# A hybrid decoder step on one core: queries and keys of the second mixer by 32 x 32 tiles, with the key features kept in the order the tiles leave them

## The reference, cut to what matters

```python
def headwise(u, w):          # 512 blocks of 4 features
    return jnp.einsum('btni,noi->btno', u.reshape(B, T, 512, 4), w).reshape(B, T, 2048)
q = headwise(xc, wq); k = headwise(xc, wk); v = headwise(xm, wv)
...
S = jnp.einsum('bhtk,bhsk->bhts', qc, kc) * W
num = w_c[..., None] * jnp.einsum('bhtk,bhkv->bhtv', qc, C) + jnp.einsum('bhts,bhsv->bhtv', S, vc)
den = w_c * jnp.einsum('bhtk,bhk->bht', qc, n) + jnp.sum(S, axis=-1)
C_new = wL_c[..., None, None] * C + jnp.einsum('bhs,bhsk,bhsv->bhkv', wL, kc, vc)
n_new = wL_c[..., None] * n + jnp.einsum('bhs,bhsk->bhk', wL, kc)
```

## Time and profile before

| what | value |
|---|---|
| median of 3 runs | 1989.37 us (1975.0 to 1992.24) |
| the profiled execution | 1977.75 us, span 1975.5 us |
| PE busy | 1763.8 us, 89% of the span |
| DVE, ACT, POOL busy | 769.9, 416.1, 192.0 us |
| mean granted PE clock | 0.929 |
| HBM read and written | 281.78 and 70.03 MB |

### The profile page before, as it was taken

The page is one execution under the profiler, slowest core; times in us unless marked ns, Lnnn a source line. Parts: engine busy times, 40 slices in busy tenths (PEclk is TensorE's granted clock), DMA queues, the critical chain, the costliest instruction groups (busy, mean ns, idle before and its releaser), DMA issues.

```text
span 1975.5 us, 24262 instructions
## 1 busy us (share of the span) xinstructions
PE 1763.8 (89%) x9638; PEld 1296.4 (66%) x9638; DVE 769.9 (39%) x1662; ACT 416.1 (21%) x649; POOL 192.0 (10%) x294
## 2 busy tenths in 40 slices
PE   6999999997969997898969999899998998889983
PEld 3777777765758885676744664646646776778863
DVE  1244444444142111655665644555544004221104
ACT  3233233321131111311131221311211003011111
POOL 0000000000011221000003003021030000112110
PEclk9999899988979998898979989998999998889996
DMA  8444444453238998311116419054182221679923
GB/s 351 140 161 146 144 150 150 150 192 132 74 110 270 385 361 320 130 54 43 49 52 249 156 35 349 22 213 181 43 300 91 67 72 70 210 235 364 368 81 144
DMA packets 95843, 336.48 MB, mean 170 GB/s; under 512 B 15824, under 2 KB 15824, under 8 KB 94976
## 3 DMA queue, kind: packets, MB, share of 16 engines
q1 hardware_dynamic: 63648, 234.13, 33.4%
q0 software_dynamic: 32096, 100.96, 13.8%
HBM read 281.78 MB, written 70.03 MB: 178 GB/s over the span
## 4 chain that ended last, share of the span: by engine, by line
PE 78%; DVE 10%; DMA 5%; ACT 4%; issue 3%; POOL 0%; DVEq 0%; SPq 0%; ACTq 0%; POOLq 0%
PE ps L575 29%; PE ps L878 13%; PE ps L884 6%; PE ps L677 4%; PE ps L587 2%; PE ps L1178 2%; PE ps L597 2%; PE ps L1151 2%; PE ps L1099 2%; PE ps L890 2%; PE ps L1134 1%; PE ps L1124 1%; DMA out_mc_s<-ring 1%; PE ps L632 1%; DMA ring<-in_c 1%
## 5 line engine op out<-in xcount | busy, mean ns | idle before, releaser
L575 PE MATMUL ps<-hT,ring 128*128 128x288 f32 x1792 | 463.6, 420 | 16.8 <-ACT hT L1241 11.2
L575 PEld LDWEIGHTS ps<-hT,ring 128*128 128x128 f32 x1792 | 351.2, 197 | 123.5 <-issue 15.2
L878 PEld LDWEIGHTS ps<-arena,ring 128*128 128x128 f32 x2048 | 241.6, 198 | 21.0 <-issue 14.4
L878 PE MATMUL ps<-arena,ring 128*128 128x128 f32 x2048 | 242.6, 281 | 6.6 <-DVE arena L1835 5.3
L575 PE MATMUL ps<-arena,ring 128*128 128x288 f32 x768 | 190.7, 412 | 4.0 <-DVE arena L2233 4.0
L575 PEld LDWEIGHTS ps<-arena,ring 128*128 128x128 f32 x768 | 148.5, 194 | 46.1 <-DVE arena L2233 4.5
L1842 DVE TENSOR_TENSOR arena<-ps,arena 128x128 f32<-128x128 f32 x64 | 18.6, 291 | 285.0 <-ACT arena L1354 284.9
L884 PE MATMUL ps<-ring,arena 128*128 128x512 f32 x256 | 114.8, 592 | 0.0
L884 PEld LDWEIGHTS ps<-ring,arena 128*128 128x128 f32 x256 | 46.3, 190 | 46.9 <-issue 46.9
L1598 DVE SCALAR_TENSOR_TENSOR xT<-ps,modt,xT 128x288 f32<-128x288 f32 x16 | 8.3, 518 | 172.7 <-PE ps L575 172.7
L677 PE MATMUL ps<-ring,hT 128*128 128x128 f32 (+1 forms) x640 | 73.7, 275 | 1.0 <-DVE arena L1676 1.0
(11 more groups left out here) (423 smaller groups left out, 2273.6 us busy)
## 6 DMA issues: line engine op xcount, KB each, us to landing
ring<-in_wstream SPq DMA_DIRECT2D x376, 512.0 KB, 5.7
ring<-in_c SPq DMA_DIRECT2D x32, 512.0 KB, 6.5
arena<-in_c SPq DMA_DIRECT2D x32, 512.0 KB, 7.2
out_mc_s<-arena POOLq DMA_DIRECT2D x64, 256.0 KB, 5.2
out_mc_s<-ring POOLq DMA_DIRECT2D x64, 256.0 KB, 6.7
arena<-in_wstream POOLq DMA_DIRECT2D x24, 512.0 KB, 9.2
arena<-y_rows POOLq DMA_DIRECT2D x8, 1024.0 KB, 8.3
arena<-in_hg POOLq DMA_DIRECT2D x8, 512.0 KB, 3.9
```

What stands on the lines that cost most here:

```text
L575: mm = pe.matmul(ps[:, 2 * p + half, 0:TH], ring[:, r, c * P:(c + 1) * P], rhs(k)[:, TH * half:TH * (half + 1)], start=(k == 0), stop=(k = ...
L878: mm = pe.matmul(ps[:, n // 2, P * (n % 2):P * (n % 2 + 1)], w[:, P * c:P * (c + 1)], rows[:, c, :], start=(c == 0), stop=(c == DC - 1))
```

## The change

Queries and keys are made by 16 tiles of 32 rows by 32 columns instead of eight matrices of 128 x 128. The 128 inputs of chunk i split into four row groups r; row group r of chunk i goes to column group c = (r + i) mod 4, so that four row groups of one i hit four column groups and each row group has its own bank r. What bank r holds on partitions of column group c is therefore chunk (c - r) mod 4, row group r: the features of queries and keys of a head lie in another order. `head_weights` makes two products of 128 x 128 numbers in place of eight. The 64 sample tokens of both go to banks 0 to 3. ACT and DVE share the evictions, 512 prompt tokens of two chunks in one instruction.

Keys by token are no longer made from `xc`: PE transposes the evicted, scaled keys in `ml["kz"]`, so they wait for the evictions. The scores wait for their eviction in two parts. The last product of a head is made in two instructions, and the next head's first query eviction waits for the first alone.

The states follow the new order. Each load from DRAM and each store, per key block r, splits into the pieces of `key_parts`: partitions 32r to 128 take chunks 0 to 3 - r, partitions 0 to 32r the rest. A load is seven transfers in place of two, a store seven in place of four, the prompt's state blocks are seven in place of four per head. The DRAM side of a piece is a list of chunks by 32 rows by 512 values. The old normalizers are copied into the order by 16 small DVE copies, and the new ones leave in 16 transfers in place of one.

```diff
-N_HEADB = 26
+N_HEADB = 20
...
+HALF_PARTS = (3, 4)
+def key_parts(r):
+    return [(slice(BLK * r, P), slice(0, 4 - r))] + ([(slice(0, BLK * r), slice(4 - r, 4))] if r else [])
...
+        def key_tiles(tensor, r):
+            chunks = tensor.rearrange("p (i v) -> i p v", i=HT)
+            return [(rows, chunks[which, BLK * r:BLK * (r + 1), :]) for rows, which in key_parts(r)]
...
-                        sp.wait_ge(c_out[n % 4][half], 32 * (n // 4))
-                    sp.dma_start(states[n % 4][:, of_half], io["c0"][n][:, of_half]).then_inc(state_in(n, half)[0], 16)
+                        sp.wait_ge(c_out[n % 4][half], 16 * HALF_PARTS[half] * (n // 4))
+                    for r in (2 * half, 2 * half + 1):
+                        for rows, src in key_tiles(io["c0"][n], r):
+                            sp.dma_start(states[n % 4][rows, MD * r:MD * (r + 1)], src).then_inc(state_in(n, half)[0], 16)
...
-                        pool.dma_start(part_of(out["mc_s"][n], k), part_of(states[n % 4], k)
-                                       ).then_inc(c_out[n % 4][k // 2], 16)
+                        for rows, dst in key_tiles(out["mc_s"][n], k):
+                            pool.dma_start(dst, states[n % 4][rows, MD * k:MD * (k + 1)]).then_inc(c_out[n % 4][k // 2], 16)
...
+            def tiles_of(h, w, bank, at_out, tokens):
+                n = tokens.stop - tokens.start
+                for i in range(HT):
+                    for r in range(4):
+                        c = (r + i) % 4
+                        rows = slice(BLK * r, BLK * (r + 1))
+                        mm = pe.matmul(ps[BLK * c:BLK * (c + 1), bank + r, at_out:at_out + n], bdq[rows, w, i, :],
+                                       ml["xc"][rows, HT * h + i, tokens], start=True, stop=True, skip_group_check=True)
+                return mm
...
+            def keys(h):
+                pe.wait_ge(s["quad_read"].sem, 4 * h + 2)
+                s["quad_full"].on(tiles_of(h, 1, 4, 0, slice(0, TP)))
...
+                if h:
+                    queries(h)
+                for p in range(2):
+                    pe.wait_ge(pair_free[p].sem, (hb + 2) // 2)
+                whole_row(0)
+                if h:
+                    keys(h)
+                whole_row(1)
...
+                pe.wait_ge(s["quad_read"].sem, 4 * h + 4)
                 for j in range(4):
                     for i in range(HT):
-                        mm = pe.matmul(ps[:, 4 + j, P * i:P * (i + 1)], ml["xc"][:, HT * h + i, P * j:P * (j + 1)],
-                                       bdq[:, (HT + i) * P:(HT + i + 1) * P], start=True, stop=True)
-                s["kt_full"].on(mm)
+                        mm = pe.transpose(ps[:, 4 + j, P * i:P * (i + 1)], ml["kz"][:, i, P * j:P * (j + 1)], ident)
+                    if j % 2:
+                        s["kt_full"].on(mm)
+                whole_row(2)
...
+            def queries_read(r):
+                s["quad_read"].on(act.copy(ml["q"][:, r:r + 2, 0:TP], ps[:, 4 + r:6 + r, :]))
+            def keys_read(r):
+                s["quad_read"].on(act.activation(ml["kz"][:, r:r + 2, 0:TP], ps[:, 4 + r:6 + r, :], ACT.Identity, scale=KS))
...
+                if h + 1 < MH:
+                    dve.wait_ge(s["quad_full"].sem, 3 * h + 5)
+                    pair_free[0].on(dve.tensor_copy(q[:, :, TP:T], ps[:, 0:4, 0:64]))
+                    pair_free[1].on(ts(z[:, :, TP:T], ps[:, 0:4, 64:128], KS, None, ALU.mult))
+                    s["quad_read"].on(dve.tensor_copy(q[:, 2:4, 0:TP], ps[:, 6:8, :]))
+                    dve.wait_ge(s["quad_full"].sem, 3 * h + 6)
+                    s["quad_read"].on(ts(z[:, 2:4, 0:TP], ps[:, 6:8, :], KS, None, ALU.mult))
```

More of the change, by code:

```diff
@@ L403, in _ @@
                 for half in range(2):
[L404 removed]
+                    sp.wait_ge(c_out[2 + u][half], 16 * HALF_PARTS[half] * (NB * MH // 4))
                     entry(RING["md"] + 4 + 2 * u + half, RING["md"] - 3)
@@ L1037, in _, with queries @@
             weighted = [mx[f"P{j}"] for j in range(4)]
-            bdq = ml["W"].rearrange("p a b -> p (a b)")
-            def queries_and_keys(h):
+            def tiles_of(h, w, bank, at_out, tokens):
[7 more added lines that the diff above has]
+                return mm
+            def queries(h):
                 pe.wait_ge(s["bd_ready"].sem, h + 1)
+                pe.wait_ge(s["c_done"].sem, HT * NB * h)
+                s["quad_full"].on(tiles_of(h, 0, 4, 0, slice(0, TP)))
+                for p in range(2):
+                    use()
                 for w in range(2):
[L1043 to L1048, removed]
+                    mm = tiles_of(h, w, 0, 64 * w, slice(TP, T))
+                s["quad_full"].on(mm)
+            def keys(h):
+                pe.wait_ge(s["quad_read"].sem, 4 * h + 2)
+                s["quad_full"].on(tiles_of(h, 1, 4, 0, slice(0, TP)))
+            queries(0)
+            keys(0)
+            pe.wait_ge(s["quad_read"].sem, 4)
             pe.wait_ge(s["rows_ready"].sem, 1)
@@ L1072, in row_of, with whole_row @@
                             ml["rows"][32 * k:32 * k + MH, :])
+                def whole_row(k):
+                    p = use()
+                    full.on(wide((2 * p, 2 * p + 1), *([x] for x in row_of(k))))
+                if h:
+                    queries(h)
+                for p in range(2):
+                    pe.wait_ge(pair_free[p].sem, (hb + 2) // 2)
[3 more added lines that the diff above has]
+                whole_row(1)
+                pe.wait_ge(s["cp_ready"].sem, HT * h)
                 p = use()
@@ L1095, in _ @@
                     hi = TP if j < 4 else T
-                    for p in range(2):
-                        pe.wait_ge(pair_free[p].sem, (hb + 8) // 2)
+                    if j in (0, 2):
+                        pe.wait_ge(s["kt_read"].sem, 2 * h + j // 2 + 1)
                     for i in range(HT):
@@ L1445, in _ @@
             s["dec_exp"].on(act.activation(gb[:, TP:T], gb[:, TP:T], ACT.Exp))
-            for i in range(6, 8):
-                query_or_key(i)
             act.wait_ge(x_kept, 16)
@@ L2095, in _ @@
             ub = USES["b"]
-            n0 = col("n0", MT, NB)
+            n0 = col("n0", MH, HT, NB)
+            for r in range(HT):
+                for c in range(4):
+                    ins = dve.tensor_copy(n0_keys[BLK * c:BLK * (c + 1), :, r, :], n0[BLK * r:BLK * (r + 1), :, (c - r) % 4, :])
+            V.link(dve, ins)
             for h in range(MH):
@@ L2215, in _ @@
                 if h + 1 < MH:
-                    for u in range(2):
-                        dve.wait_ge(cp_out[u], 8 * HT * (h + 1))
+                    dve.wait_ge(cp_out[0], 16 * HALF_PARTS[0] * (h + 1))
                     head_weights(h + 1)
```

137 lines of the change are left out of this document (74 added, 63 removed).

## The result

The changed kernel took 2207.07 us, median of four runs (2201.36 to 2211.79), against 1984.16 for the kernel before on the same chips (1975.0 to 1992.24): ratio 1.1143, 95% interval 1.1103 to 1.1183. Slower, as forecast, and for the loads by the mechanism forecast, but 67 us above the 2140 and 22 above the range.

A forecast was written before the change was run, and what follows sets the result against it. PE was taken as the bound, with a state's store and load setting the sample loop's end. 1977.75 - 22 (head starts) + 180 (state transfers on few engines) = 2136, said as 2140 us by the median; own range 2075 to 2185.

The forecast's parts named there:

- What bounds the kernel: Whole kernel: PE busy 89% of the span; in the sample loop, a state's store and load already set the end.
- Part 5, Spread: Sample loop: state pieces led by 4, 3 or 2 chunks use only that many DMA engines; +180 us (120 to 200).
- the price taken: Sample loop: +45 us per head for few engines carrying the state pieces, between +30 and +49.
- Part 5, the stores: Sample loop: seven stores and the prompt's state also want the fullest engine, 8 x 2.4 = 19 us.
- Part 5, Issue and Bytes: State transfers: more issues cost +3 us per head (0 to 5), POOL not binding; 2 KB load runs cost nothing.
- rival 1: State pieces spread over all 16 engines, only issue costs of 4 x 3 remain: 1979 us by the median; chance 0.18.
- Parts 1 to 4: Head starts: tiles, evictions, turned keys and the first head together save 22 us (10 to 29).
- Part 2: Head start: evictions and their order, ScalarE and VectorE side by side; keys end at 6.1, sample key rows at 8.2.
- Part 1: Head start: queries and keys by 32 x 32 tiles; 32 records take 1.1 us if sixteen run together, otherwise 3.6.
- rival 3: Head start: tiles do not run sixteen at once, keys 2.5 us later per head, 1976 us; chance 0.05.
- Part 3: Head start: keys by token from 16 transposes, 2.0 us instead of 3.84; first score at 11.5, 6 us less per later head.
- Rival 2: State pieces on all 16 engines, full DMA engines hide the longer issue: 1956 us, faster; chance 0.13.

The follow-up runs named there:

- the leading count alone: Kernel before, DRAM side of its two state loads written as 16, 4 or 2 lists, pieces unchanged: 1983.34, 2105.58 and 2276.27 us.
- stores by rows: Changed kernel, its seven state store pieces written in plain DRAM row order, loads as changed: 2163.68 us.
- both by rows: Changed kernel, its seven load and seven store pieces all in plain DRAM row order: 1996.15 us, ratio 1.0094 to the kernel before.
- the host's order: Changed kernel, states put into key order by the host, two load and four store transfers as before: 1959.36 us, ratio 0.9924 to the kernel before.
- loads led by 2: Kernel before, DRAM side of each state load written as 2 lists of 64 rows: 2276.27 us.
- stores led by 4: Kernel before, DRAM side of each state store written as 4 lists of 32 rows, loads unchanged: 2083.5 us.

## Why the prediction came out as it did

**What bounds the kernel** held: store and load of a state set the loop, and the change spent 247 us there. The upper bound of 2185 was added up wrongly: its own terms give 1977.75 + 200 - 10 + 11.6 = 2179. The measured time lies above both.

**Part 5, Spread: right for the loads.** The chosen end, few engines, is shown by the leading count alone and by its plateaus of 4 and 2 engines. Its sum holds where it can be read alone: with stores by rows the four loads took 75.1 us from first issue to last landing (1055.55 to 1130.64), against 54.4 + 19 = 73.4, and sample 7 stood 82.5 us into the loop (1048.15 to 1130.69), where the price taken puts it at 35.7 + 45 = 80.7. The Trainium skill (DMA: Bandwidth & Descriptors, Why a DMA increments its semaphore by 16 and not by 1) gives this count for SP's transfers, and the shares of 0.26 and 0.13 agree with it.

**Part 5, the stores: the step that failed.** "Seven stores and the prompt's state want that engine as well, 14/16 of a share each: 8 x 2.4 = 19 us" prices a list-led store like an even one, and the +45 taken leaves out part of even that (+49 with all of it). A list-led store costs more engine time for its bytes. POOL's queue in the first loop of the changed kernel (1054 to 1140), then with stores by rows (1055 to 1131):

```profile
q0 software_dynamic: 10570, 7.95, 42.8%
```

```profile
q0 software_dynamic: 2768, 7.86, 32.4%
```

That is 13.5 GB/s for an engine's busy time against 20.0 with the same pieces led by rows; the step from 24.8, with four stores a state, down to 20.0 belongs to the seven pieces. The chain with stores by rows, and SP's first loads there:

```profile
1051.98 3.14 POOL out_mc_s L556 x6
1055.13 2.98 DMA out_mc_s<-arena
```

```profile
1055.55 29.68 SPq L398 DMA_DIRECT2D arena<-in_c  x14
```

Two things follow, and the two traces show both. From POOL's first store to SP's first load it takes 9.0 us in the changed kernel (1048.23 to 1057.19) and 3.6 with stores by rows (1051.98 to 1055.55), so the first load goes out 12.8 us into the loop, not 7.4; and the four loads beside the slower stores take 83.5 us (1057.19 to 1140.67), not 75.1. That is 13.8 us in head 0. Over the four loops the lists in the stores cost 50 us (loops of 100.0 and 87.3 in the mean), and another 16 is what even stores exceeded the price taken (87.3 against 38.3 + 45): together the 66 by which the loops missed their 180.

**Part 5, Issue and Bytes: wrong where they stood, without effect on the forecast.** The forecast of few engines did not add them; rival 1 did, at 3 us a head for issues and nothing for bytes. Seven even pieces cost 8.2 us a head (loops of 46.6 against 38.4 in the mean), by the rate and not by the issues. "POOL does not bind" is right. Rival 1, whose condition both by rows sets up, would have been 1996 and not 1979, and outside its 1958 to 1990.

**Parts 1 to 4** made 18.4 us of the 22 in the changed kernel (4.7 and 13.7), and 15 (9 to 21) by themselves. Head 0: 4.7 against 4, but that is one pair of executions: its first score lies between 1024.63 and 1033.13 in the six kernels here with the old head start and between 1022.92 and 1030.97 in the eight with the new one, 3.1 us apart in the mean. The start of a later head saved 4.6 us by the table, 3.8 from the product's start to the first score in head 2, and not 6. Part 2 was right: product, evictions and tiles came within 0.3 us of their steps, and keys ended 6.4 us after the product's start (6.1 forecast). Part 1's sixteen tiles run together: 32 records took 1.63 us, nearer to 1.1 than to 3.6, so rival 3 falls. The loss is in Part 3: the sample keys by token (L1129, 1.08 us) stand behind the rows, so the transposes begin at 9.6, not at 8.2, and take 3.19 us, not 2.0. The forecast took the row of transposes at a granted clock of 1.00; the trace of before also has eight in 1.97 us at a clock of 0.50 (L965, 1933.30). See below.

**Rival 2** (seven pieces on all engines, the longer issue hidden) did not come: both by rows took 1996. Its 1956, the saving alone, is what the host's order gives, 1959, where the pieces are two and four again. Between the loops nothing was late, as forecast, not even with loads led by 2.

The waits were forecast at some 17 us a sample. Those at the read, 23.1, 8.4, 12.2 and 9.5 us at samples 4 to 7, are fewer; PE stands idle 11 to 14 us of each 20 from 1084 on, and part of that is before other instructions than the read. The fall of the DMA share came as forecast, but from 1084 on alone.

## What to carry to other kernels

A reordering that costs nothing on the compute engines can cost more than ten times its gain in the transfers that must follow it: look at the leading dimension of both sides of each new access pattern, and keep it a multiple of 16 (here lists of 2 and 4 cost much, 16 little or nothing). The sign to look for is a DMA share that falls while an engine waits for DMA; and a full DMA share proves no rate, read GB/s beside it. If the new order can be given to the data outside, as here, the gain stays.

## What the runs showed that was not expected

**Small packets of list-led stores.** Each store of POOL led by A adds 16 x (16 - A) packets under 512 B: 192 per store with A = 4 (24,576 for 128 stores). For the changed kernel's pieces led by 4, 3, 2, 2 and 3 that makes 192 + 208 + 224 + 224 + 208 = 1056 a state, 38,016 for 32 states and the four of the prompt, and 56,512 less the 18,496 of the run with stores by rows is 38,016. The Trainium skill (DMA: Bandwidth & Descriptors, Why a DMA increments its semaphore by 16 and not by 1) says that on POOL's queue a transfer uses its few engines from a place that moves on and that all 16 post its end; the share of 0.84 fits that better than a fixed four. The small packets are not the cost by themselves. In the packet records of the run with stores led by 4 they have 8 bytes and take 9 ns each, some 37 us in the stretch of 1055 to 1110, of the 561 us of engine time (63.8% of 16 engines for 55 us) that POOL's queue took there. What grew is the time of its packets of 4096 bytes: 302 ns in the mean, against 163 in the kernel before (1050 to 1090), with a median of 159 in both, so some of them take very long. What holds those up is open.

**SP's issues under few engines.** A load issue took 0.33 us in the median before (L379) and four took 1.75. In the changed kernel the median is 2.1 to 2.3 us and the longest 8.75. With the same seven pieces and both sides by rows it is 0.58. So the chain's SPq is not SP's own work on more pieces: an issue grows long where few engines carry the loads.

**The clock at a head's start.** The changed kernel's PE stands 3.30 us for the evictions in the middle of head 2's start, which has little work left for it. Stretches of the changed kernel, then of the kernel before over the same step:

```profile
1373.00:1380.00 7.00, 3.70 (x96) 1.74 (x80) 5.08 (x7) 1.90 (x3) 0.00 (x0) 0.89 0.56 181
1380.00:1387.00 7.00, 7.00 (x42) 4.92 (x40) 3.85 (x8) 2.71 (x3) 0.00 (x0) 0.62 0.05 19
```

```profile
1270.00:1276.00 6.00, 6.00 (x56) 4.99 (x54) 0.00 (x0) 1.41 (x3) 0.00 (x0) 1.00 0.01 3
```

The granted clock is 0.62 behind the pause, mostly the lower level of 1.2 GHz, where it was 1.00. There the 16 transposes take 199 ns each, and 130 in the earlier trace rows at a clock of 1.00. So part of what shorter work saves at the start is given back by the clock: 1.1 us of 16 transposes, by 16 x 69 ns.
